# Where the cached pages of a sparse-attention decoder layer are asked for: gathers on GpSimd, or register-addressed DMAs on SyncE

## What is computed

```python
# indexer: which 256 of the 1028 keys each sample query may see
ki_past = pool_ki[page_table].reshape(db, past, IDX_DIM)
sel = top_k(where(pos_k <= pos_q, sum_h w[q,h] * relu(qi[q,h] . ki[l]), NEG_INF), 256)
# attention over the selected keys and values of the paged cache
ks, vs = pool_k[rows(sel)], pool_v[rows(sel)]       # rows through the page table
attn = softmax(q . ks / 8) @ vs
# then: output projections, gated residual, and per token 128 experts,
# each one row of peer_u (a dot product) and one row of peer_v (added up)
```

## Time and profile before

| | us |
|---|---|
| median of 3 runs (lowest, highest) | 1168.03 (1166.55, 1168.33) |
| span of the profiled execution, first to last instruction | 1087.7 |
| median less span | 80.3 |
| last of VectorE's rounds ends | 261 |
| sample values begin | 278.16 |
| expert rows: DMA engines full | 354 to the end |

### The profile page before, as it was taken

The page is one execution under the profiler, slowest core; times in us unless marked ns, Lnnn a source line. Parts: engine busy times, 40 slices in busy tenths (PEclk is TensorE's granted clock), DMA queues, the critical chain, the costliest instruction groups (busy, mean ns, idle before and its releaser), DMA issues.

```text
span 1087.7 us, 11138 instructions
## 1 busy us (share of the span) xinstructions
PE 954.1 (88%) x3288; PEld 487.3 (45%) x3288; DVE 717.1 (66%) x1782; ACT 415.6 (38%) x1120; POOL 380.1 (35%) x410
## 2 busy tenths in 40 slices
PE   4999999998999999999999887877877777777787
PEld 2457877654777555554444332322232222222222
DVE  1366879886547877676677888888864444444544
ACT  2112313111303555455466444345344444433343
POOL 0374051771001333343334333333333333333330
PEclk9999999998999999999999999899999999999999
DMA  9854262984536999999999999999999999999994
GB/s 368 356 203 154 78 229 90 350 300 179 196 135 256 412 392 421 421 421 421 421 421 421 421 421 421 423 420 421 421 421 421 422 421 422 422 420 423 422 421 168
DMA packets 52497, 380.06 MB, mean 349 GB/s; under 512 B 7139, under 2 KB 7315, under 8 KB 11094
## 3 DMA queue, kind: packets, MB, share of 16 engines
q0 software_dynamic: 46016, 312.90, 70.0%
q1 hardware_dynamic: 6134, 66.11, 15.6%
q10 hardware_dynamic: 288, 0.35, 0.1%
HBM read 377.75 MB, written 1.59 MB: 349 GB/s over the span
## 4 chain that ended last, share of the span: by engine, by line
DMA 42%; PE 40%; DVE 11%; ACT 4%; issue 2%; POOL 0%; DVEq 0%; SPq 0%; ACTq 0%; POOLq 0%
DMA big<-peer_uv,oT 35%; PE twoD L958 8%; PE twoD L960 7%; PE twoA L593 5%; PE twoA L897 4%; DMA r<-peer_uv,oT 4%; PE twoA L571 3%; DVE big L1585 3%; PE twoD L831 3%; DMA big<-weight_rows 3%; DVE best L1582 3%; DVE big L1842 2%; PE twoD L819 1%; ACT big L1281 1%; ACT oT L1276 1%
## 5 line engine op out<-in xcount | busy, mean ns | idle before, releaser
L1072 POOL DMA_INDIRECT big<-peer_uv,oT x259 | 244.4, 944 | 491.4 <-PE twoD L960 370.1
L958 PE MATMUL twoD<-big 128*128 128x512 f32 x518 | 285.9, 634 | 93.7 <-ACT big L1281 93.5
L1842 DVE CUSTOM_DVE_ANT_0 big<-big,twoA 128x1024 f32<-128x1024 f32 x146 | 178.2, 1221 | 144.3 <-DMA big<-peer_uv,oT 143.1
L960 PE MATMUL twoD<-big 128*128 128x512 f32 x518 | 268.9, 601 | 0.0
L1276 ACT ACTIVATE oT<-oT,wsel 128x1 f32<-128x1 f32 x288 | 84.4, 293 | 317.8 <-DVE oT L1842 314.1
L958 PEld LDWEIGHTS twoD<-big 128*128 128x128 f32 x518 | 85.3, 191 | 265.0 <-ACT big L1281 226.1
L1842 DVE CUSTOM_DVE_ANT_0 big<-big,twoD 128x1024 f32<-128x1024 f32 x113 | 137.9, 1221 | 69.5 <-DMA big<-peer_uv,oT 68.2
L960 PEld LDWEIGHTS twoD<-big 128*128 128x128 f32 x518 | 99.9, 193 | 126.6 <-issue 126.6
L1281 ACT ACTIVATE big<-ctab,oT 128x128 f32<-128x128 f32 x288 | 115.6, 401 | 9.5
L593 PE MATMUL twoA<-hT,big 128*128 128x288 f32 x448 | 113.1, 409 | 0.0
L593 PEld LDWEIGHTS twoA<-hT,big 128*128 128x128 f32 x448 | 83.6, 190 | 25.9 <-issue 4.2
(11 more groups left out here) (340 smaller groups left out, 999.2 us busy)
## 6 DMA issues: line engine op xcount, KB each, us to landing
big<-weight_rows SPq DMA_DIRECT2D x24, 2048.0 KB, 11.2
big<-weight_rows SPq DMA_DIRECT2D x8, 1024.0 KB, 5.1
big<-peer_uv,oT POOLq DMA_INDIRECT x259, 22.6
r<-weight_rows SPq DMA_DIRECT2D x1, 2048.0 KB, 11.9
big<-weight_rows SPq DMA_DIRECT2D x1, 1312.0 KB, 15.8
xT<-token_rows SPq DMA_DIRECT2D x1, 1152.0 KB, 8.0
out_y_prompt<-r SPq DMA_DIRECT2D x2, 512.0 KB, 7.7
r<-key_rows,key_at POOLq DMA_INDIRECT x40, 5.6
```

The lines of the kernel that those rows point to most:

```text
L958: pe.matmul(acc[0][:, :], diag[j % NDG], row[:, 0:512], start=(s == 0), stop=(s == SLOTS[t] - 1), skip_group_check=True)
L960: mm = pe.matmul(acc[1][:, :], diag[j % NDG], row[:, 512:D], start=(s == 0), stop=(s == SLOTS[t] - 1), skip_group_check=True)
L1072: pool.indirect_dma_start(pairs[home[i]], None, peer_uv, bass.IndirectOffsetOnAxis(ap=eidx[:, t, s:s + 1], axis=0)).then_inc(row_in[home[i ...
L1842: dve.tensor_tensor_reduce(out=row, in0=row, in1=h2tok[t][:, :], scale=1.0, scalar=0.0, op0=ALU.mult, op1=ALU.add, accum_out=dots[:, t, s: ...
```

## The change

All 192 pages are asked for by SyncE, one DMA each. For every page SyncE loads the page number from the table in SBUF into a register (`value_load`, L973), tests its bounds, works out the row, and asks for a plain DMA with that address. The gathers go from GpSimd, the row numbers from VectorE. The pages stand at four places in the order of the weights:

- behind conv 0: 64 index pages and the 8 key pages of sequence 4;
- behind gate 1: the keys of 5 and 6 (16 pages), after the wait on `scored[0]`;
- behind convout: the keys of 0 to 3 and 7 (40 pages), after `attended[0]` and `a_ready`;
- before out 0, behind attnout: the 64 value pages, after adaG 10 and adaG 11 are released.

```diff
+            def page_number(b, g):
+                return sp.value_load(pages[0:1, NPG * b + g:NPG * b + g + 1], min_val=0, max_val=NPHYS - 1)
+            def load_index(b):
+                for g in range(NPG):
+                    q, v = g // 2, g % 2
+                    sp.dma_start(ibT[v * HD:(v + 1) * HD, b, q, :], index_rows[bass.ds(page_number(b, g) * HD, HD), :]).then_inc(i_landed[b], 16)
...
+            def load_values(b):
+                for g in range(NPG):
+                    rows = vpages[g * (P // NPG):(g + 1) * (P // NPG), b * NPG:(b + 1) * NPG].rearrange("p g d -> p (g d)")
+                    sp.dma_start(rows, value_rows[bass.ds(page_number(b, g) * (P // NPG), P // NPG), :]).then_inc(v_landed, 16)
+            def load_keys(b):
+                for g in range(NPG):
+                    sp.dma_start(keys_of(b)[:, g * PAGE:(g + 1) * PAGE], key_rows[bass.ds(page_number(b, g) * P, P), :]).then_inc(k_landed[b], 16)
...
                 if g == group("out"):
+                    sp.wait_ge(*released[group("adaG", 0)])
+                    for b in range(4, NB):
+                        load_values(b)
+                    sp.wait_ge(*released[group("adaG", 1)])
+                    for b in range(4):
+                        load_values(b)
                     sp.wait_ge(*v_done[1])
...
+                if g == group("conv"):
+                    sp.wait_ge(in_pages, 16)
+                    for b in range(NB):
+                        load_index(b)
+                    load_keys(4)
+                if g == group("gate", 1):
+                    sp.wait_ge(*scored[0])
+                    load_keys(5)
+                    load_keys(6)
+                if g == group("convout"):
+                    sp.wait_ge(*attended[0])
+                    for b in range(KB):
+                        load_keys(b)
+                    sp.wait_ge(a_ready, 1)
+                    load_keys(NB - 1)
```

More of the change, by code:

```diff
@@ L243, in layer_program @@
         pages = sb("pages", [P, NB * NPG], I32)
-        page_rows = sb("page_rows", [P, NB], I32)
-        key_at = sb("key_at", [P, NB * NPG], I32)
-        index_at = sb("index_at", [P, NB * 4], I32)
         NK = 5
@@ L379, in layer_program @@
         in_front, in_x, in_pages, in_const = sem("in_front"), sem("in_x"), sem("in_pages"), sem("in_const")
-        in_ident, page_rows_ready = sem("in_ident"), sem("page_rows_ready")
+        in_ident = sem("in_ident")
         w_landed = [sem(f"w_landed{i}") for i in range(7)]
@@ L641, in _ @@
                             if half == v == 0:
-                                pe.wait_ge(i_landed[bb], 16 * 4)
+                                pe.wait_ge(i_landed[bb], 16 * NPG)
                             at8 = sbank[half][32 * b4:32 * b4 + 32, :].rearrange("r (q v p) -> r v q p", q=2, v=2)
@@ L779, in sample_values @@
                     pe.wait_ge(probsT_ready, 6 + 3)
-                pe.wait_ge(v_landed, 16 * NB)
+                pe.wait_ge(v_landed, 16 * NB * NPG)
                 b = V.open(pe)
@@ L972, in _ @@
             sp.dma_start(xT[:, :, :].rearrange("p c t -> p (c t)"), token_rows).then_inc(in_x, 16)
+            def page_number(b, g):
[4 more added lines that the diff above has]
+                    sp.dma_start(ibT[v * HD:(v + 1) * HD, b, q, :], index_rows[bass.ds(page_number(b, g) * HD, HD), :]).then_inc(i_landed[b], 16)
+            value_rows = cache_v.rearrange("(r e) d -> r (e d)", e=NPG)
+            def load_values(b):
[5 more added lines that the diff above has]
+                    sp.dma_start(keys_of(b)[:, g * PAGE:(g + 1) * PAGE], key_rows[bass.ds(page_number(b, g) * P, P), :]).then_inc(k_landed[b], 16)
             for g, name in enumerate(names):
@@ L1014, in _ @@
             pool.memset(uP[:, :, 0:2], 0.0).then_inc(consts_ready, 1)
[L1015 to L1030, removed]
             for n, (t, k_out, v_out, i_out) in enumerate((
@@ L1040, in _ @@
                 pool.dma_start(i_out, zbuf[0:r, t, Z_KI:Z_KI + HD]).then_inc(kv_out, 16)
[L1041 to L1051, removed]
             def ask(i):
@@ L1381, in _ @@
             L.tell(cp(rep_bf[:, :], cv["rep"][0:NSM, :]), wait=False)
[L1382 to L1395, removed]
             L.tell(dve.memset(stat[:, 0:30], 1.0))
```

## The result

| measured together | this, us | the kernel before, us | ratio (95% interval) |
|---|---|---|---|
| changed kernel, first measurement | 1188.23 (1187.35 to 1189.65) | 1168.05 | 1.0175 [1.0161, 1.019] |
| changed kernel, second occasion | 1187.69 (1186.64 to 1189.52) | 1088.74 | 1.0916 [1.0897, 1.0935] |
| changed kernel, third occasion | 1187.85 (1186.32 to 1188.58) | 1160.75 | 1.0225 [1.0198, 1.0251] |

The kernel before has two levels of time, about 1088 and 1161 to 1168 us. All its executions that were timed together were at one of them, and from one occasion to another it changed; the changed kernel was at 1186 to 1190 us on all three. The trace ahead of the prediction is of the short level, the times that stand beside it are of the long one.

What follows compares the result with a forecast made beforehand. The first 340 us were taken to decide when the byte-bound expert part begins. Waits of 27.1 + 34.1 + 46.3 = 107.5 us plus 14 for the clock gave 121.5 more: 1289.5 us, 8-in-10 range 1216 to 1430.

Steps and rivals of the forecast that it cites:

- What bounds the kernel: Whole span: expert rows from 354 us live on bytes, untouched by the change; only when that second part may begin counts.
- The base: Start of the sum: span 1087.7 us, median 1168.03 us, with 80.3 us taken as outside the span and left unchanged.
- place 2: Behind convout: 40 key pages delay the weight of gate 6, so PE waits 40c - 15.9 = 34.1 us.
- place 3: Behind attnout: 64 value pages delay the sample values, which wait 64c - 33.7 = 46.3 us.
- the clock: Behind the three long PE waits: lower granted clock costs 5 + 5 and 4 us, 14 us in all.
- place 1: Behind conv 0: 64 index and 8 key pages delay conv 1's weight, so PE waits 72c - 62.9 = 27.1 us.
- c: SyncE time of one page, register load, register instructions and DMA issue together: taken as 1.25 us, ends 0.47 and 2.34.
- (a) to (d): Rival page prices in us: 1.7 to 2.34, chance 0.2; 0.5 to 0.89, 0.1; about 0.47, 0.03; below 0.45, 0.02.
- What goes "at nothing": On GpSimd and VectorE: removing 104 gathers and 12 small instructions, both off the path, was costed at nothing.

## Why the prediction was wrong

**What bounds the kernel.** Right. The part from the sample values on has its length in every kernel here, and all of the difference lies ahead of it.

**The base: wrong, and the step that failed.** "The span was 1087.7, the median 1168.03 with 80.3 outside the span, which I leave as it is." Outside the span lie 1.75 us. Of the 80.3, the other 78.5 were the stops of the longer level, inside the span, in executions that had not been profiled, and they belong to gathers that this change takes away. I had written the 80.3 down as an assumption and given it no rival, namely that the times and the profile were of executions of two kinds. A sum that was made for the 1088 level was added to a time of 1168 us. Made against its own level, it gives a span of 1087.7 + 121.5 = 1209.2 us, 21.3 over the 1187.9 measured; the range, shifted likewise, would have held it. So of the 100 us between the 1289.5 forecast and the 1189.65 of the profiled execution, 78.5 are the base and 21.3 the terms of the sum: 5.3 in place 2, 10.3 in place 3 and 7 in the clock, less 1.2 in place 1. That the change came out slower on the occasion of the first measurement too is no proof of the sum: at that level +20 us is the difference of two large effects, of which the prediction knew one.

**Place 1 (27.1 us): right.** 28.3. Conv 1 was asked for at 121.8, as 31 + 72c says, was used 7.7 us later where the sum had 7.6, and the waits for index pages lay inside.

**Place 2 (34.1 us): right mechanism, mis-sized.** 28.8, and 40 x 1.12 - 15.9 = 28.9. The term c was one value for all; it is 1.27 for an index page and 1.12 for a key page, since a DMA of 64 rows holds the queue 0.47 us and one of 128 rows 0.33.

**Place 3 (46.3 us): right mechanism, mis-sized.** The distance from gate 6's block to the values grew from 59.0 us (219.15 to 278.16) to 96.5: 37.5, of which 1.5 are gate 6's block at the low clock (5.60 for 4.15). That leaves 36.0, and 64 x 1.10 - 33.7 is 36.7.

**The price c (1.25 us): right within 12%.** Its parts were not. The register load costs about 0.5 us from its start to the next instruction, not 0.38, and the bounds test 0.29 of a page, not the 0.18 of two register instructions. The issue was put at 0.47; the DMA instruction is busy that long for an index page alone, and 0.33 and 0.32 for keys and values. These errors go both ways, so that 1.25 came so near is in part luck. With c at 1.10 to 1.27 the prices of all rivals, (a) to (d), are ruled out.

**The clock (14 us): half.** 7.03 for 4.05 us in conv 1's block, 5.60 for 4.15 in gate 6's and some 2.5 from the values on: 7 us. Stage rows behind the waits (busy times, then PEclk, DMA share and GB/s at the end) show why:

```profile
130.00:134.00 4.00, 4.00 (x10) 2.74 (x9) 0.00 (x0) 0.00 (x0) 0.00 (x0) 0.50 0.97 414
134.00:138.00 4.00, 4.00 (x20) 2.14 (x18) 0.00 (x0) 0.41 (x1) 0.00 (x0) 0.83 1.02 438
...
279.00:283.00 4.00, 3.86 (x10) 2.88 (x11) 3.56 (x6) 0.00 (x0) 0.00 (x0) 0.61 1.03 442
283.00:287.00 4.00, 4.00 (x23) 3.32 (x22) 3.56 (x5) 0.61 (x2) 0.00 (x0) 1.00 0.99 422
...
374.00:378.00 4.00, 2.35 (x45) 2.38 (x49) 0.00 (x0) 0.00 (x0) 0.00 (x0) 0.50 0.06 20
378.00:382.00 4.00, 4.00 (x95) 3.13 (x88) 0.35 (x1) 0.00 (x0) 0.00 (x0) 0.61 0.00 0
```

The low level of 1.2 GHz lasted one to two stretches, where I had carried over the three of the earlier trace rows. Keeping PE at work gave 3.9 us back in the medians, so how much of the 7 reaches the end is not settled. In the traces the parts are 28.3 + 28.8 + 36.0 + 7 = 100.1 of the 100.2; the 36.0 was itself found by subtraction, so this is a division of the 100.2 and no test of it. The tests are the prices: 36.7 for that part, and the 51.6 us of the run without the bounds test.

**What goes "at nothing".** Right at the 1088 level: 101 us less of GpSimd brought nothing. Wrong at the other, and this is the second half of the failed step: there the gathers cost 79 us of TensorE's and ScalarE's time without any wait that names them, and +99 less 79 is the +20 of the first measurement.

## What to carry to other kernels

Where the median and the span of the profiled execution differ by more than a few microseconds, the profile may be of another kind of execution than the times: find out, by the span of the timed ones, before a sum made from the one is added to the other. Small transfers that move to a queue which serves a fixed order of weights cost what stands behind them, pages x (price of one) less the cover; spread between the weights the same pages cost 33.6 us less, and 24 of them with cover nothing. When the issue time counts, look at the bounds test of each load: leaving it out took 51.6 us off. Testing the whole table once outside the loop would be the safe form of it; no run here shows what that costs.

## What had not been expected of the hardware

- A kernel of one core has two levels, 1088 and 1161 to 1168 us, constant through an occasion. Chip 8 was at 1088 on one and at 1168 on another, so it is not the chip alone. The gathers of 512-byte rows started 1.25 us apart at either.
- While these gathers run at the longer level, PE starts one matmul in 2.8 us in the first stop and none for 40 us in the last, and ScalarE nothing for 35, 14 and 41 us. VectorE is idle in the first and goes on with its rounds in the last. The large expert gathers later, with 1 MB each, do nothing of the kind: that part is 809.4 us for 809.5.
- Two register instructions that are busy 0.17 us cost a loop of loads 0.29 us a turn (0.28 for value pages).
- A plain DMA holds SyncE's queue 0.47, 0.33 or 0.32 us, for 64 rows of 512 bytes, 128 rows of 512 bytes and 16 rows of 4 KB.
